# Four pairs of PSUM banks for the first score steps of two softmax attentions

## The reference

```
s = einsum('bqghd,bkgd->bghqk', qi, k_win) * scale - slopes * (t - sp)
p = masked_softmax(s, sp <= t)
o = einsum('bghqk,bkgd->bqghd', p, v_win)
out = g[...,0]*o_cmp + g[...,1]*o_slc + g[...,2]*o_win
y = x + (o * silu(z)) @ w_out
```

## Time and profile before

| what | value |
|---|---|
| median of 3 runs | 1478.77 us (1477.15 to 1480.62) |
| the profiled execution's own time | 1475.55 us |
| its span | 1473.4 us |
| PE busy | 1439.2 us (98%) |
| DVE busy | 959.5 us (65%) |
| ACT busy | 872.0 us (59%) |
| fox attention | about 980 to 1022 us of the span |
| nsa attention | about 1275 to 1424 us |

### The profile page before, as it was taken

The page is one execution under the profiler, slowest core; times in us unless marked ns, Lnnn a source line. Parts: engine busy times, 40 slices in busy tenths (PEclk is TensorE's granted clock), DMA queues, the critical chain, the costliest instruction groups (busy, mean ns, idle before and its releaser), DMA issues.

```text
span 1473.4 us, 25052 instructions
## 1 busy us (share of the span) xinstructions
PE 1439.2 (98%) x10188; PEld 934.1 (63%) x10188; DVE 959.5 (65%) x1928; ACT 872.0 (59%) x1254; POOL 65.7 (4%) x150
## 2 busy tenths in 40 slices
PE   7999999999999999999999999999999999899998
PEld 4444477566468448576689764646685755466677
DVE  6732556888589666565677423677667246799974
ACT  6554456777654665454563653557665466778863
POOL 0000000000000100000010000102000000000000
PEclk9999999999999999999999999999999999999999
DMA  6323233113322424342323223321024432100002
GB/s 193 111 90 114 86 97 103 59 58 115 114 87 86 161 86 129 108 137 87 114 87 114 88 87 101 102 86 34 29 88 131 132 116 86 58 2 2 2 4 99
DMA packets 128530, 131.93 MB, mean 90 GB/s; under 512 B 9912, under 2 KB 125408, under 8 KB 128288
## 3 DMA queue, kind: packets, MB, share of 16 engines
q1 hardware_dynamic: 126096, 121.62, 25.7%
q0 software_dynamic: 2320, 8.71, 1.7%
HBM read 128.18 MB, written 2.10 MB: 88 GB/s over the span
## 4 chain that ended last, share of the span: by engine, by line
PE 80%; DVE 14%; ACT 3%; issue 1%; DMA 1%; SPq 0%; POOL 0%; DVEq 0%; ACTq 0%
PE bank L730 13%; PE bank L731 13%; PE bank L732 13%; PE bank L773 8%; PE bank L775 8%; PE bank L774 8%; DVE tmin L2499 4%; DVE scr L2517 2%; DVE bank L2495 2%; PE bank L899 1%; DVE wring L1951 1%; PE bank L917 1%; PE bank L1037 1%; PE bank L1133 1%; PE bank L853 1%
## 5 line engine op out<-in xcount | busy, mean ns | idle before, releaser
L730 PE MATMUL bank<-xT,whigh 128*128 128x512 f16 x952 | 360.9, 379 | 1.1 <-DVE wring L1951 1.1
L732 PE MATMUL bank<-xT,wring 128*128 128x512 f16 x952 | 360.8, 379 | 0.0
L731 PE MATMUL bank<-xT,whigh 128*128 128x512 f16 x952 | 360.8, 379 | 0.0
L1951 DVE SCALAR_TENSOR_TENSOR wring<-wring,wsc,whigh 128x2048 f16<-128x2048 f32 (+2 forms) x106 | 245.2, 2314 | 136.6 <-ACT whigh L1322 135.9
L1322 ACT ACTIVATE whigh<-wring,wsc 128x2048 f16<-128x2048 f32 (+2 forms) x106 | 209.0, 1972 | 121.3 <-DVE wsc L1854 97.2
L1339 ACT ACTIVATE whigh<-wring 128x2048 bf16<-128x2048 f32 (+2 forms) x106 | 199.1, 1878 | 92.5 <-DMA wring<-in_w_down 27.2
L773 PE MATMUL bank<-whigh,slab 128*128 128x256 f16 x800 | 218.0, 273 | 2.2 <-DVE wring L1951 1.6
L775 PE MATMUL bank<-whigh,slab 128*128 128x256 f16 x800 | 218.1, 273 | 0.0
L774 PE MATMUL bank<-wring,slab 128*128 128x256 f16 x800 | 218.0, 273 | 0.0
L730 PEld LDWEIGHTS bank<-xT,whigh 128*128 128x128 f16 x952 | 93.1, 98 | 113.3 <-issue 2.7
L732 PEld LDWEIGHTS bank<-xT,wring 128*128 128x128 f16 x952 | 93.2, 98 | 112.4
(11 more groups left out here) (336 smaller groups left out, 2301.8 us busy)
## 6 DMA issues: line engine op xcount, KB each, us to landing
wring<-in_w_in SPq DMA_DIRECT2D x27, 1024.0 KB, 5.1
wring<-in_w_up SPq DMA_DIRECT2D x16, 1024.0 KB, 5.3
wring<-in_w_down SPq DMA_DIRECT2D x16, 1024.0 KB, 5.2
wring<-in_even_w_in SPq DMA_DIRECT2D x14, 1024.0 KB, 5.3
wring<-in_odd_w_in SPq DMA_DIRECT2D x14, 1024.0 KB, 5.2
wring<-in_w_a SPq DMA_DIRECT2D x4, 1024.0 KB, 5.2
wring<-in_w_out SPq DMA_DIRECT2D x4, 1024.0 KB, 5.3
wring<-in_even_w_out SPq DMA_DIRECT2D x4, 1024.0 KB, 5.1
```

Source lines behind the costliest of these rows:

```text
L730: pe.matmul(bank, wh[:, k, wcol:wcol + width], xh[:, k, :], start=k == 0, stop=False)
L731: pe.matmul(bank, wh[:, k, wcol:wcol + width], xl[:, k, :], start=False, stop=False)
L732: mm = pe.matmul(bank, wl[:, k, wcol:wcol + width], xh[:, k, :], start=False, stop=k == KC - 1)
L1951: dve.scalar_tensor_tensor(low_of(i)[:, :, 0:m], loaded(i)[:, :, 0:m], wsc[:, n:n + 1], high_of(i)[:, :, 0:m], ALU.mult, ALU.subtract).the ...
```

## The change

Four things, in both attentions:

- The first four score steps get four different pairs of banks. Pair p is banks 2p and 2p+1. Fox uses pairs 0, 2, 3, 1 for steps 0 to 3, nsa pairs 0, 1, 2, 3. From step 4 on it is pair 0 and pair 1 in turn, as before.
- On PE, S(4) is issued right behind S(3), ahead of T(0); so the first turns are S(0), S(1), S(2), S(3), S(4), T(0), then T(1), V(0), then S(5), T(2), V(1), and so on.
- The waits follow: S(2) and S(3) wait for no exp. In nsa S(2) waits for the gate's last eviction (`zo_ev` 8) and S(3) for the copy of the compressed probabilities (`ct_ev` 16, which V's turn waited for before). In fox S(1) no longer waits for the gate's last eviction (`ze_ev` 8), and S(3) does. S(4) and S(5) wait for the first user of pair 0 and pair 1. T(0) waits for the exp of the step that used pair 2 (fox: exp(1), nsa: exp(2)), V(0) for that of the step that used pair 3 (fox: exp(2), nsa: exp(3)).
- On DVE `bound_behind(.., 7)` moves from the end of turn 1 to the end of turn 5.

```diff
--- before.py
+++ after.py
@@ -510,8 +510,21 @@
         TPB = ps[4:6]
         OB = ps[6:8]
 
-        def scores(i, e):
-            return bank[:, 2 * (i % SCORE_SLOTS) + e, :]
+        FIRST_PAIRS = {"fox": (0, 2, 3, 1), "nsa": (0, 1, 2, 3)}
+
+        def bank_pair(n, i):
+
+            return FIRST_PAIRS[n][i] if i < 4 else i % SCORE_SLOTS
+
+        def first_use(n, pair):
+
+            return FIRST_PAIRS[n].index(pair) + 1
+
+        def scores(n, i, e):
+            return bank[:, 2 * bank_pair(n, i) + e, :]
+
+        def both_scores(n, i):
+            return bank[:, 2 * bank_pair(n, i):2 * bank_pair(n, i) + 2, :]
 
         def probs(i, e, w):
             slot = 2 * (i % PROB_SLOTS) + e
@@ -927,38 +940,48 @@
             def attention(A):
 
                 n, steps, N = A.name, A.steps, len(A.steps)
-                for i in range(N + VALUE_LAG):
+
+                def step_scores(i):
                     if i == 0:
                         gate = {"fox": "ze", "nsa": "zo"}[n]
                         pe.wait_ge(s_(gate + "_ev"), n_(gate + "_ev", 6))
-                    if i == 1:
+                    if i == 1 and n == "nsa":
+                        pe.wait_ge(s_("cs_ev"), 16)
+                    if i == 2 and n == "nsa":
+                        compressed_turn(7)
+                        pe.wait_ge(s_("zo_ev"), n_("zo_ev", 8))
+                    if i == 3:
                         if n == "fox":
                             pe.wait_ge(s_("ze_ev"), n_("ze_ev", 8))
                         else:
-                            pe.wait_ge(s_("cs_ev"), 16)
-                    if i == 2 and n == "nsa":
-                        compressed_turn(7)
-                        pe.wait_ge(s_("zo_ev"), n_("zo_ev", 8))
-                    if i == VALUE_LAG and n == "nsa":
-                        pe.wait_ge(s_("ct_ev"), 16)
-                    if i < N:
-                        m, b, parts = steps[i]
-                        if i >= SCORE_SLOTS:
-                            pe.wait_ge(s_(n + "_ex"), n_(n + "_ex", i - SCORE_SLOTS + 1))
-                        for t, c in parts:
-                            w = (t + 1) * P
-                            for e in range(2):
-                                rows, row = A.bias(m, e, w)
-                                pe.matmul(scores(i, e)[:, c:c + w], rows, row, start=c == 0, stop=False)
-                        for t, c in parts:
-                            w = (t + 1) * P
-                            for e in range(2):
-                                mm = pe.matmul(scores(i, e)[:, c:c + w], A.q(2 * m + e, t), A.k(2 * m + e, b, w), start=False, stop=t == parts[-1][0])
-                        mm.then_inc(s_(n + "_sc"), 1)
+                            pe.wait_ge(s_("ct_ev"), 16)
+                    if 4 <= i < 6:
+                        pe.wait_ge(s_(n + "_ex"), n_(n + "_ex", first_use(n, i - 4)))
+                    if i >= 6:
+                        pe.wait_ge(s_(n + "_ex"), n_(n + "_ex", i - SCORE_SLOTS + 1))
+                    m, b, parts = steps[i]
+                    for t, c in parts:
+                        w = (t + 1) * P
+                        for e in range(2):
+                            rows, row = A.bias(m, e, w)
+                            pe.matmul(scores(n, i, e)[:, c:c + w], rows, row, start=c == 0, stop=False)
+                    for t, c in parts:
+                        w = (t + 1) * P
+                        for e in range(2):
+                            mm = pe.matmul(scores(n, i, e)[:, c:c + w], A.q(2 * m + e, t), A.k(2 * m + e, b, w), start=False, stop=t == parts[-1][0])
+                    mm.then_inc(s_(n + "_sc"), 1)
+
+                for i in range(N + VALUE_LAG):
+                    if i < N and i != 4:
+                        step_scores(i)
+                    if i == 3:
+                        step_scores(4)
                     if TURN_LAG <= i < N + TURN_LAG:
                         s = i - TURN_LAG
                         for e in range(2):
                             pe.wait_ge(s_(n + "_pn"), n_(n + "_pn", 2 * s + e + 1))
+                            if s == 0:
+                                pe.wait_ge(s_(n + "_ex"), n_(n + "_ex", first_use(n, 2)))
                             if s >= 1:
                                 pe.wait_ge(s_(n + f"_te{e}"), n_(n + f"_te{e}", s))
                             for j in range(width(steps[s][2]) // P):
@@ -969,6 +992,8 @@
                         m, b, parts = steps[s]
                         ob = [OB[m % 2][e * HD:e * HD + HD, :] for e in range(2)]
                         first = b == 0 and parts == TILES[0]
+                        if s == 0:
+                            pe.wait_ge(s_(n + "_ex"), n_(n + "_ex", first_use(n, 3)))
                         if first:
                             if m >= 2:
                                 pe.wait_ge(s_(n + "_y"), n_(n + "_y", m - 1))
@@ -1662,7 +1687,7 @@
                                 act.wait_ge(s_(n + f"_tp{e}"), n_(n + f"_tp{e}", i - PROB_SLOTS + 1))
                             for part, (t, c) in enumerate(parts):
                                 cc = slice(c, c + (t + 1) * P)
-                                ins = act.activation(probs(i, e, SEQ)[:, cc], scores(i, e)[:, cc], ACT.Exp, scale=-1.0,
+                                ins = act.activation(probs(i, e, SEQ)[:, cc], scores(n, i, e)[:, cc], ACT.Exp, scale=-1.0,
                                                      bias=pair_stat(tmin, i, part, e), accum_out=pair_stat(tsum, i, part, e))
                         ins.then_inc(s_(n + "_ex"), 1)
                     if i == 1 and n == "nsa":
@@ -2491,12 +2516,12 @@
                     if i < N:
                         dve.wait_ge(s_(n + "_sc"), n_(n + "_sc", i + 1))
                         for t, c in steps[i][2]:
-                            last = bank[:, 2 * (i % SCORE_SLOTS):2 * (i % SCORE_SLOTS) + 2, c + t * P:c + (t + 1) * P]
+                            last = both_scores(n, i)[:, :, c + t * P:c + (t + 1) * P]
                             ins = dve.tensor_tensor(last, last, future[:, :].unsqueeze(1).to_broadcast([P, 2, P]), ALU.add)
                         ins.then_inc(dve_chain, 1)
                         dve.wait_ge(dve_chain, own(dve_chain))
                         for part, (t, c) in enumerate(steps[i][2]):
-                            ins = dve.tensor_reduce(pair_stat(tmin, i, part), bank[:, 2 * (i % SCORE_SLOTS):2 * (i % SCORE_SLOTS) + 2, c:c + (t + 1) * P],
+                            ins = dve.tensor_reduce(pair_stat(tmin, i, part), both_scores(n, i)[:, :, c:c + (t + 1) * P],
                                                     AX_X, ALU.min)
                         ins.then_inc(s_(n + "_dm"), 1)
                     if 1 <= i < N + 1:
@@ -2517,7 +2542,7 @@
                                     ins = dve.tensor_scalar(pr, pr, pair_stat(trec, s, part, e), gates[:, t, 3 * h + 1 + b:3 * h + 2 + b],
                                                             ALU.mult, ALU.mult)
                             ins.then_inc(s_(n + "_pn"), 1)
-                    if i == 1:
+                    if i == 5:
                         bound_behind({"fox": "ze", "nsa": "zo"}[n], 7)
                     if i == 2 and n == "nsa":
                         after("zo", 3)
```

## The result

The changed kernel takes 1481.99 us in the median of 14 runs (1479.85 to 1484.42), the kernel before 1477.20 us in 14 runs beside them (1474.69 to 1480.65). The ratio is **1.0035**, 95% interval 1.0027 to 1.0042: 5.2 us slower (1477.2 x 0.0035), between 4.0 and 6.2; the medians lie 4.8 apart. Forecast were 4.6 us and a time of 1483.4, which started from a median of 1478.8 for the kernel before.

What follows compares the result with a forecast made beforehand. DVE was taken to bound both attentions. Nsa +3.5 us (2.1 + 0.79 + 0.57) and fox +1.1 sum to 4.6, on a median of 1478.8: 1483.4 us, range 1479.4 to 1486.0.

Steps and rivals of the forecast that it cites:

- The bound of the stage: Both attentions: DVE is the bound, so PE's idle time there costs nothing by itself.
- POOL's answer: End of turn 5, both attentions: DVE stalls 0.57 us for it, as the reader now stands directly behind the bound.
- S(3), C(0) and S(5): Start of nsa: S(3) waits for the copy (PE idle 4.1 us), C(0) for exp(3), DVE for S(5) ahead of add(5).
- the moved bound: Both attentions: 0.79 us leave turn 1 and come back at the end of turn 5; the move by itself is worth 0.
- Fox: The fox attention: +1.1 us, from +0.4 at full clock to +2.3 with half clock under T(1), V(0) and S(5).
- Nsa: The nsa attention: 2.1 + 0.79 + 0.57, +3.5 us, of 1.36 to 4.4.
- the half clock: Nsa, after PE's idle time: 0.50 under S(3), S(4) and T(0), add(5) 1.5 to 3.05 us late, 2.1 taken.
- its return under V(0) and S(5): Rival: half clock outlasts S(5) in both attentions or falls again; 3 us more than 6.7, up to 1488.5; chance 0.05.
- the new terms: Nsa at full clock: whole gain gone at add(5), then 0.79 and 0.57 after it, 1.36 us later.
- the spans between the attentions differ: Sign between the attentions: the prediction is wrong if these spans differ from before.
- the lower bound: Low end of the range, 1479.4: the full-clock rival (1480.6 to 1481.7, chance 0.32) less 1 us for scatter.
- The advice of the Trainium skill: By it, using all 8 PSUM banks would gain; cited under the rival that PE is the bound, 1473.8 us, chance 0.05.

Runs made afterwards that it cites:

- k: The change with the bound at the end of turn 4, S(5) of nsa ahead of V(0), and 26 extra matmuls ahead of S(3) of nsa; ratio 0.9994.
- j: The kernel before with extra bias matmuls in PE's idle times ahead of S(2) and S(4) in both attentions; ratio 0.9997.
- l: The kernel before, filled as in j, with the bound still in turn 1 but ahead of the reciprocal of step 0; ratio 1.0000.
- b: The kernel before with only the bound moved to the end of turn 5, banks and PE's order unchanged; ratio 1.0005.
- a: The change with the bound put back at the end of turn 1; ratio 1.0020.
- h: The change with the bound at the end of turn 4, one turn earlier; ratio 1.0016.
- d: The change in the nsa attention alone, fox as in the kernel before; ratio 1.0027.
- g: The change with S(5) of nsa issued ahead of V(0), behind T(1), fox as in the change; ratio 1.0013.
- f: The change with three pairs of banks (0, 1, 2, 1) for nsa's first steps and the waits adapted; ratio 1.0017.
- e: The change with 14 extra bias matmuls in nsa just ahead of S(2), which overwrites their results; ratio 1.0020.
- c_fox_only: The change in the fox attention alone, nsa with banks, order, waits and bound of the kernel before; ratio 1.0009.

## Why the prediction was right

- **The bound of the stage.** "An idle time of PE in these stages costs nothing by itself" held: PE's idle time of 2.87 us ahead of S(2) went and brought nothing, since DVE had not waited for it. With a full clock nsa took the same 18.20 us in the new order (k) and in the old (j): DVE's own work sets it, with 0.2 us of waiting that only l took away.
- **POOL's answer.** 0.57 us forecast for each attention; 0.50 of idle time and 0.67 more in nsa measured (b).
- **S(3), C(0) and S(5).** The waits came where they were put: 4.15 us for the copy (4.1), one for exp(3) ahead of C(0), DVE's wait for S(5) in both. That this wait swallows what DVE had won, so that the moved bound is paid in full, was confirmed by a (1.44 us in nsa, 1.36 forecast); h fits, but at another clock.
- **Fox:** +1.1 forecast, +1.39 in the profile, 1.3 us (0 to 2.7) as 0.09% in the runs. Its lower end of +0.4 was reckoned from the 17.14 us of the profile before, which held 0.4 us of half clock; with a full clock on both sides it is +0.60 (17.32 less 16.72).
- **Nsa**: +3.5 forecast. The runs give 0.27%, 4.0 us (2.5 to 5.5). In the profile it was 5.15, over the upper end of 4.4. **The term that was mis-sized is the half clock**: I let it lie under S(3), S(4) and T(0) and gave its return under V(0) and S(5) a chance of 0.05. It returned there in three of the profiles (the change, a, d) and not in g, h and f. In the runs of the change and of d it came in about half, if the two groups of times are read so; that isn't shown. With a full clock the new terms cost 1.7 (e), not 1.36. That the sum of 4.6 still came within 0.6 us of 5.2 is in part luck: the runs are a mixture of cases, and their ratio lies between them.
- The prediction also said that it would be wrong if the spans between the attentions differ. They did, by 1.66 us, through one fall of the clock at unchanged code, which executions of the old order show as well. So this sign was badly chosen: it can't tell a wrong prediction from the scatter.
- Small slips in its numbers: the lower bound, 1480.6 less 1, is 1479.6 and not 1479.4, and the upper end of the forecast, 1478.8 + 6.7, is 1485.5, not 1486.0. The result lies inside either way.
- What I had overlooked: the old order has too little slack for a half clock at the wrong place. I read its harmlessness from one profile. In c_fox_only it cost the old order 3.4 us in nsa.
- The advice of the Trainium skill, "Perfetto Trace Analysis", section "Matmul Optimizations", to use all eight PSUM banks, brought nothing here. All eight were in use before, two pairs of them for T and V, so the change only used them in another order. The fourth pair for scores was lent by V(0) and by the copy, and both came back as waits: nsa is 19.10 us with three pairs and 23.37 with four (the half clock has a part in that difference), the ratios are 1.0017 and 1.0035.

## What to carry to other kernels

Lending a buffer of a later stage to an earlier one makes the later stage wait for its last reader; look at what is queued behind that wait on the same engine, here S(5) behind V(0). A small operation whose answer takes a trip through another engine wants a turn of other work between it and its reader, and the best place for it is where its engine waits anyway. And where the granted clock of the same code differs from one execution to the next, as here, one profile shows one of several cases. Compare several before you call an order's slack enough. Filling the idle time kept the clock full in the starts of these attentions, but it didn't make the kernel before faster in the median.

## What the runs showed of the hardware

- The granted clock fell to 0.50 (1.2 GHz) after idle times of 2.16 (before, d), 2.26 (c), 2.87 (before) and 2.90 us (the change), and stayed full after 2.16 (b), 2.48 (c), 2.64 (e) and 2.89 us (g). The pairs of 2.16, and of 2.90 and 2.89, lie at the same place of fox. Idle time of about the same length at the same place was thus followed by either clock. The length of the idle time alone doesn't tell it.
- The clock also fell with no idle time of PE in the rows ahead of it: in 8 of the 13 profiles under the transposes behind 32 matmuls of 31 columns (2.50 us), in the change after 20 us with PE busy throughout at 1.00 (1223.7 to 1243.7).
- The clock stayed at 0.50 over 9.8 us with PE busy in all of them (c). The other rows of it shown here are 3.0 to 6.8 us long.
- Extra bias matmuls of 512 columns with 64 rows each, in turn on the upper and lower rows, took about 0.11 us each (14 of them in 1.52 us in e_warm, from 1280.67 to 1282.19), half of the 0.22 us from start to start of the projections' matmuls of 512 columns with 128 rows.
- With the idle times in the starts filled, 11 runs spread over 2.2 us in j, but over 3.4 in l; the 21 and 15 runs of the kernel before beside them spread over 5.3 and 3.5. So the starts of the attentions aren't the whole cause of the scatter, and the fall in the compressed branch is one more. Time and clock go together run by run: of the kernel before beside a, b, g and h, 13 runs with a mean clock of 0.996 took 1476.2 us on average, 12 with 0.995 took 1477.5. Which place fell in each isn't on record.
